# Sliding-window attention on one core: four groups of eight blocks run as one sequence of 32, with the stages of a block one block further apart

## The reference

```python
q = rms_norm((rms_norm(x, g_norm) @ w_q).reshape(b, s, 16, 64), g_q)   # 16 heads, 4 share a key head
logits = einsum("bntkgd,bnskd->bnkgts", q, k_band) * 64 ** -0.5        # 128 tokens see 256 keys
logits = where(mask, logits - slopes * dist, -inf)                     # ALiBi bias, window of 128
m = maximum(max(logits), sink)
p = exp(logits - m)
denom = sum(p) + exp(sink - m)
o = einsum("bnkgts,bnskd->bntkgd", p / denom, v_band)
x = x + o.reshape(b, s, 1024) @ w_o
```

## Time and profile before

| What | Value |
|---|---|
| median of 3 runs | 2092.54 us (2092.04 to 2097.11) |
| the profiled execution | 2095.45 us, its span 2093.5 us |
| PE busy | 2005.1 us, 96% of the span |
| DVE busy | 1400.6 us, 67% |
| ACT busy | 909.2 us, 43% |
| POOL busy | 407.5 us, 19% |
| mean granted TensorE clock | 0.986 |

### The profile page before, as it was taken

How to read it: one execution, slowest core, us unless ns; L and a number is a source line. 1 busy time by engine, 2 the same in 40 slices (tenths; PEclk the granted TensorE clock), 3 DMA queues, 4 the chain that set the end, 5 groups by cost and what they waited for, 6 DMA issues and landing times.

```text
span 2093.5 us, 29024 instructions
## 1 busy us (share of the span) xinstructions
PE 2005.1 (96%) x9968; PEld 1694.9 (81%) x9968; DVE 1400.6 (67%) x2050; ACT 909.2 (43%) x1560; POOL 407.5 (19%) x285
## 2 busy tenths in 40 slices
PE   7999899999999999999998789879899999999999
PEld 7988678788888888888998677757788888888887
DVE  5366568888887854444553777879887887853433
ACT  6233335444444443333313677746444444433332
POOL 0000001432333200001111444422333333200000
PEclk9999899999999999999999999999999999999999
DMA  4111232122221254333120000012222221254533
GB/s 165 41 51 40 71 123 98 73 89 80 80 93 68 105 219 177 131 140 111 32 69 31 11 21 10 10 61 81 81 81 79 88 92 60 110 221 150 189 139 113
DMA packets 44719, 192.96 MB, mean 92 GB/s; under 512 B 4336, under 2 KB 4464, under 8 KB 32368
## 3 DMA queue, kind: packets, MB, share of 16 engines
q1 hardware_dynamic: 44656, 192.12, 25.2%
HBM read 156.45 MB, written 35.65 MB: 92 GB/s over the span
## 4 chain that ended last, share of the span: by engine, by line
PE 84%; DVE 11%; ACT 2%; issue 2%; DMA 0%; POOL 0%; DVEq 0%; SPq 0%; ACTq 0%; POOLq 0%
PE banks L1933 28%; PE banks L1935 27%; PE banks L1934 27%; DVE lg L1847 2%; DVE t_lo L1461 1%; DVE pT_lo L1796 1%; DVE t_sum L1653 1%; DVE t_sum L1451 1%; ACT o_hi L1142 1%; DVE o_lo L1804 1%; DVE fw_lo L1443 1%; DVE small L1854 0%; DVE xT L1543 0%; DVE fw_lo L1504 0%; PE banks L2301 0%
## 5 line engine op out<-in xcount | busy, mean ns | idle before, releaser
L1933 PE MATMUL banks<-t_hi,fw_hi 128*128 128x512 f32 x1760 | 688.5, 391 | 12.7 <-issue 11.1
L1935 PE MATMUL banks<-t_hi,fw_lo 128*128 128x512 f32 x1760 | 686.1, 390 | 0.0
L1934 PE MATMUL banks<-t_lo,fw_hi 128*128 128x512 f32 x1728 | 674.0, 390 | 0.0
L1933 PEld LDWEIGHTS banks<-t_hi,fw_hi 128*128 128x128 f32 x1760 | 331.4, 188 | 86.5 <-issue 14.4
L1935 PEld LDWEIGHTS banks<-t_hi,fw_lo 128*128 128x128 f32 x1760 | 331.4, 188 | 69.1
L1934 PEld LDWEIGHTS banks<-t_lo,fw_hi 128*128 128x128 f32 x1728 | 325.2, 188 | 67.7 <-issue 0.5
L1599 DVE TENSOR_TENSOR fw_lo<-raw,fw_hi 128x512 fp32r<-128x512 f32 x120 | 84.4, 705 | 189.2 <-ACT fw_hi L979 189.2
L580 POOL TENSOR_TENSOR nrm<-raw 128x512 f32<-128x512 f32 x40 | 53.6, 1340 | 753.9 <-DVE fw_lo L1504 439.6
L932 ACT ACTIVATE xT<-xT,par 128x1024 f32<-128x1024 f32 x88 | 109.3, 1245 | 161.5 <-DVE xT L1530 119.0
L979 ACT ACTIVATE fw_hi<-raw 128x512 fp32r<-128x512 f32 x120 | 75.6, 631 | 210.6 <-PE banks L1935 210.6
L1543 DVE SCALAR_TENSOR_TENSOR xT<-xT,par 128x1023 f32<-128x1023 f32 x88 | 151.3, 1720 | 0.0
(11 more groups left out here) (184 smaller groups left out, 3647.0 us busy)
## 6 DMA issues: line engine op xcount, KB each, us to landing
raw<-in_w_f_in SPq DMA_DIRECT2D x44, 1024.0 KB, 4.8
raw<-in_w_f_out SPq DMA_DIRECT2D x44, 1024.0 KB, 4.8
c_scratch<-xT SPq DMA_DIRECT2D x44, 512.0 KB, 2.6
c_raw<-c_scratch SPq DMA_DIRECT2D x44, 512.0 KB, 5.6
w_raw<-in_w_ao SPq DMA_DIRECT2D x16, 512.0 KB, 3.4
x_scratch<-xT SPq DMA_DIRECT2D x4, 2048.0 KB, 7.4
xT<-x_scratch SPq DMA_DIRECT2D x4, 2048.0 KB, 12.9
xT<-in_x_t SPq DMA_DIRECT2D x16, 256.0 KB, 7.1
```

Source lines behind the costliest of these rows:

```text
L1933: nc.tensor.matmul(out, w_h, m_h, start=start, stop=False, **kw)
L1934: nc.tensor.matmul(out, w_h, m_l, start=False, stop=False, **kw)
L1935: return nc.tensor.matmul(out, w_l, m_h, start=False, stop=stop, **kw)
```

## The change

- The four groups are written out, and on every engine the blocks count through from 0 to 31 (`block`). The stages of block n run over the border between groups: queries of the next group are split and turned in blocks 6 and 7 of this one.
- The next group's biases are made in block 3, by ScalarE instead of VectorE, into a second buffer. Its keys are copied in block 6 (`k_twice`), transposed and split in block 7 (`keys_transpose`, `keys_upper`, `keys_lower`).
- `o_upper` and `o_lower` move by one block (n-3 instead of n-2) and to an earlier place within the block; `pT_hi` and `pT_lo` have two buffers.
- In groups 1 to 3 TensorE's `p_transpose` stands ahead of `logits`, and `weighted` is last; in group 0 it is `logits`, `p_transpose`, `weighted`. `p_transpose` has a new wait, for `pT_ready` of the block before.
- The output tiles start one block later: blocks 6 and 7 of group 0 held four, now block 7 holds two, and behind block 7 of group 3 stand three pairs and 8 tiles instead of two pairs and 8. The splits of their weights move from blocks 4 and 6 to 5 and 7.
- On VectorE one of the two additions of a block now stands behind the reciprocals; the sinks are read from the parameters and no longer copied.
- GpSimd's `v_lower` stands behind blocks 0 and 2 instead of ahead of block 0 and behind block 1.

```diff
@@ -109,7 +109,7 @@
 def step_outs(n):
 
 
-    o = (2 * n + 4) % (2 * KT)
+    o = (2 * n + 2) % (2 * KT)
...
-        pT_hi = sb("pT_hi", [P, 2, QPK * P], F32R)
-        pT_lo = sb("pT_lo", [P, 2, QPK * P], F32R)
+        pT_hi = sb("pT_hi", [P, 2, 2, QPK * P], F32R)
+        pT_lo = sb("pT_lo", [P, 2, 2, QPK * P], F32R)
+        bias_j = [bias_0, sb("bias_1", [P, QPK, 2, P], F32)]
...
+            def core(j):
                 for n in range(NCH):
-                    if n + 2 < NCH:
-                        q_lower(j, n + 2, 3)
+                    ahead = NCH * j + n + 2
+                    if ahead < NKV * NCH:
+                        q_lower(ahead // NCH, ahead % NCH, 3)
                     probabilities(n)
-                    if n == 1:
-                        v_lower(j, 1)
-                    if first:
-                        if n == 2:
-                            split(1)
-                    else:
-                        if n == 4:
-                            split(0)
-                        if n == 6:
-                            split(1)
+                    if n in (0, 2):
+                        v_lower(j, n // 2)
+                    if j == 0 and n == 2:
+                        split(1)
+                    if j and n == 5:
+                        split(0)
+                    if j and n == 7:
+                        split(1)
...
-                if first:
-                    act.wait_ge(cols_free[1], 1 + COLS_ALL)
...
+
+                for h in range(QPK):
...
                         nc.scalar.activation(lg[:, n % 2, h, b0:2, :], lg[:, n % 2, h, b0:2, :], ACT.Exp,
                                              bias=small[:, 6, h:h + 1], accum_out=small[:, 7, h:h + 1])
                     nc.scalar.activation(small[:, 7, 4:8], small[:, 6, 4:8], ACT.Exp).then_inc(exp_done, 1)
-                    if old:
-                        o_upper((n - 2) % NCH)
-                    if n == 1:
-                        v_upper(j, 1)
-                    if first and n == 2:
+                    if n + 2 < NCH or more:
+                        q_upper((block + 2) // NCH, (block + 2) % NCH)
+                    if n in (0, 2):
+                        v_upper(j, n // 2)
+                    if j == 0 and n == 2:
                         split(1)
-                    if not first:
-                        if n < 6:
+                    if j:
+                        if n < 7:
                             o_outs.add()
 
-                        if n == 4:
+                        if n == 5:
                             act.wait_ge(out_full[1], o_outs.now(-1))
                             split(0)
+                        if n == 7:
+                            act.wait_ge(out_full[1], o_outs.now())
+                    if more:
+                        if n == 3:
+                            biases(j + 1)
                         if n == 6:
-                            act.wait_ge(out_full[1], o_outs.now())
-                            split(1)
-                    if n >= 6:
+                            k_twice(j + 1)
+                        if n == 7:
+                            keys_upper()
+                    if j and n == 7:
+                        split(1)
+                    if n == 7:
                         o_outs.add()
                     blk.add()
 
-            core(0, True)
-            loop(1, NKV - 1, [(use[0], 1), (use[1], 1), (blk, NCH), (grp, 1), (o_outs, NCH)],
-                 lambda j: core(j, False))
+            act.wait_ge(consts_done, 7)
+            biases(0)
+            keys_upper()
+            q_copy(1)
+            act.wait_ge(cols_free[1], 1 + COLS_ALL)
...
             p_upper(6)
+            o_upper(5)
+            p_upper(7, 1)
+            blk.add()
             o_upper(6)
             blk.add()
-            p_upper(7)
             o_upper(7)
...
+            def keys_lower():
+
                 dve.wait_ge(kT_hi_done, grp.add())
                 nc.vector.scalar_tensor_tensor(out=kT_lo[:, :], in0=flat(0, 2), scalar=small[:, 5, 0:1],
                                                in1=kT_hi[:, :].bitcast(F32), op0=ALU.mult,
                                                op1=ALU.subtract).then_inc(kT_ready, 1)
-                if not first:
-                    add_step_outs(0, (0,))
-                if not first:
-                    o_lower(6)
+
+            def core(j):
+                sinks = par[:, COL_SINK + j * QPK:COL_SINK + (j + 1) * QPK]
...
-                    if old:
+                    if block >= 2:
                         p_lower((n - 2) % NCH)
-                    if not first or n >= 6:
-                        add_step_outs(n, (0, 1) if n else (1,))
+                    if block >= 3:
+                        o_lower((n - 3) % NCH)
+                    outs_now = j > 0 or n == 7
+                    if outs_now:
+                        add_step_outs(n, (0,))
                     dve.wait_ge(exp_done, blk.now(1))
                     link(nc.vector.tensor_tensor(small[:, 4, 8:12], sums, sink_exp, ALU.add))
                     nc.vector.reciprocal(small[:, 4 + n % 2, 16:20], small[:, 4, 8:12]).then_inc(den_done, 1)
-                    if old:
-                        o_lower((n - 2) % NCH)
+                    if outs_now:
+                        add_step_outs(n, (1,))
+                    if more and n == 7:
+                        keys_lower()
                     blk.add()
...
             p_lower(6)
+            o_lower(5)
             add_step_outs(0)
+            p_lower(7, 1)
+            blk.add()
             o_lower(6)
+            add_step_outs(1)
             blk.add()
-            p_lower(7)
-            add_step_outs(1)
             o_lower(7)
+            add_step_outs(2)
...
-            def p_transpose(m):
+            def p_transpose(m, prior=True):
 
                 pe.wait_ge(p_done, blk.now())
+                if prior:
+                    pe.wait_ge(pT_ready, blk.now(-1))
...
                 if which == 0:
-                    if n == 0 or n == 6:
-                        slot = 1 if n == 0 else 0
+                    if n == 1 or n == 7:
+                        slot = 1 if n == 1 else 0
                         pe.wait_ge(w_ready[slot], use[slot].add())
-                    if n == 6:
-                        pe.wait_ge(o_ready, blk.now(-2))
-                    if n == 2:
-                        pe.wait_ge(o_ready, blk.now(-2))
+                    if n == 3 or n == 7:
+                        pe.wait_ge(o_ready, blk.now(-3))
...
+            def keys_transpose():
+
                 pe.wait_ge(kdup_done, grp.add())
...
+
+            def core(j):
                 for n in range(NCH):
-                    if n + 1 < NCH:
+                    block, more = NCH * j + n, j + 1 < NKV
+                    last = n == NCH - 1
+                    if more or not last:
                         q_transpose(2)
-                    if (n and not first) or n >= 6:
+                    if j or last:
                         step_out(n, 0)
-                    if not first or n >= 6:
                         step_out(n, 1)
-                    if n + 1 < NCH:
+                    if last and more:
+                        pe.wait_ge(lg_done, blk.now(1))
+                        keys_transpose()
+                    if j == 0 and not last:
                         logits(n + 1, 2)
-                    if n >= 2 or (n == 1 and not first):
-                        weighted((n - 2) % NCH, not first or n > 2)
-                    if n:
-                        p_transpose(n - 1)
+                    if block:
+                        p_transpose((n - 1) % NCH, block > 1)
+                    if j and not last:
+                        logits(n + 1, 2)
+                    if block >= 2:
+                        weighted((n - 2) % NCH, 0, block > 2)
+                    if last and more:
+                        pe.wait_ge(kT_ready, grp.now())
+                        logits(0, 2)
                     blk.add()
...
             step_out(0, 0)
-            weighted(6, True)
+            step_out(0, 1)
             p_transpose(7)
-            step_out(0, 1)
+            weighted(6)
             blk.add()
             step_out(1, 0)
             step_out(1, 1)
-            weighted(7, True)
+            weighted(7)
             blk.add()
+            step_out(2, 0)
+            step_out(2, 1)
```

135 lines of the change are left out of this document (55 added, 80 removed).

## The result

The changed kernel takes **2062.64 us** (median of 4 runs, 2059.48 to 2064.11) against 2092.86 us (4 runs, 2092.04 to 2097.11) of the kernel before on the same chip: ratio 0.985, 95% interval 0.9831 to 0.9868. On another chip it was 2063.5 us against 2092.94, ratio 0.9853 (0.9837 to 0.9868). The forecast was 2060 us, with a range of 2050 to 2077. The profiled execution took 2059.48 us with a span of 2057.7.

A forecast was written before the change was run, and what follows sets the result against it. No engine is full; chains passing between engines bound each group, with most lost at group borders. Gains 16.3 + 12.0 + 0.1 + 4.7 = 33.1 us take the median 2092.54 to 2059.4, said as 2060 us; range 2050 to 2077.

The forecast's parts named there:

- The content: Groups 1 and 2: work of one group without the remaining waits, 51.1 us, with a full block at 6.41 us.
- the slack of 1.1: Groups 1 to 3: GpSimd's low parts of v and second `w_lo` end at 2.3 to 3.0 or earlier, within 1.1 us.
- The ring: Group 0: a cycle over four engines, from one reciprocal to the next, sets the pace at 5.6 us a block.
- 2.0 for v and `w_lo`: Group 0, blocks 1 and 3: 2.0 us more for the low parts of v and the weights.
- 4 at the end: End of group 0: 4 us of keys before the next group's logits.
- 1.2 for the clock: Group 0: 1.2 us taken off the gain of 13.2 us for TensorE partly at 1.2 GHz, leaving 12.0.
- the cost of 0: Block 3: the biases, 1.7 us on ScalarE, delay nothing that matters; without that cover 1.7 us a group, 5 in all.
- The first: Group 0: TensorE at 1.2 GHz throughout, 8.0 us a block, the group at its old 62 us, 2071 us; chance 0.15.
- the 8.0 of the rival: Group 0: time of a block in us if TensorE runs at 1.2 GHz, with the turn over ScalarE's copy.
- The second: All blocks: GpSimd's product falls on the negated maximum, 7.0 us a block instead of 6.4, 2072 us; chance 0.15.
- the slack of 0.3 us: Each block: GpSimd's product ends at 1.7 us, before VectorE's negated maximum asks at 2.0.
- The third: Groups 1 to 3: straight code is fetched too slowly, at 2 us a block 2107 us; chance 0.03.

The follow-up runs named there:

- The two added lines: Changed kernel; GpSimd's low parts of v (block 2) and of the weights (block 5) wait for the next block's negated maximum: 2053.35 us, ratio 0.9805.
- the added products: Changed kernel with four more unused TensorE products of 512 columns in each of blocks 0 to 6 of group 0: 2061.26 us, ratio 0.9846.

## Why the prediction was right

**Groups 1 and 2** were to save 16.3 us and saved 15.1. The content was right: full blocks at 6.41 to 6.43, the border 9.25 for 9.15, the wait for keys 0.3 for 0.4, and the wait ahead of the transposes of p in block 6 0.7 for 1.0, by the very row that was laid out, the negated maximum beside `w_lo` (it took 2.03). The step that failed is "the two low parts of v ... which is within the slack of 1.1". v's low part in block 3 held the negated maximum for 0.94 us, and the block took 6.2 instead of 5.73. That is the largest part of the 0.6 us that a group was mis-sized. The two added lines gave back this 0.5 and the 0.9 of block 6.

**Group 0** was to save 12.0 and saved 10.6. The ring was right: 5.41 us a block for 5.6, with the negated maximum at 0.81 to 0.87 in four blocks, ending with GpSimd's product. The sum over it was not. The prediction's terms (first reciprocal at 1143.4, seven blocks of 5.6, 2.0 for v and `w_lo`, 4 at the end) add up to 1188.6 and not to the 1186.7 that it states: the 2.0 were left out. Added up rightly, group 0 would have saved 11.3 less 1.2 for the clock, 10.1 us, and the whole forecast would have been 31.2. That this is the measured figure is in part luck, since its terms miss both ways. The interval with v and `w_lo` in it took 8.73 us, 3.3 more than a free one, where 2.0 was meant. From the last reciprocal to the next logits it was 2.25 us, for 4. The 1.2 for the low clock was about right: the added products show 1.0, in the block with the biases.

**Biases, split code, group 3.** Group 3 to its last logits was to gain 0.1 and lost 0.35, the same 0.5 us of v's low part. The biases on ScalarE took 1.70 us for four (forecast 1.7). In groups 1 and 2 they held nothing up. In group 0 their block still takes 6.15 us when the clock is high, 0.7 above 5.41, and ScalarE is busy for 6.11 of it: the cost of 0 does not hold there, though in the changed kernel it is hidden behind the low clock. The loop is worth 0, measured by itself.

**Tail.** Forecast: 24.7 us from the end of the logits of block 7 to the third tile and a gain of 4.7; measured 24.4 (25.32 less 0.95 for the logits themselves) and 5.05. The wait for VectorE's addition was there with 3.1 us, for 3.2.

**Sum.** 33.1 forecast, 31.2 in the attention of the profiled pair, 30.2 between the medians. By stages the gap to 31.2 is 1.2 in groups 1 and 2, 1.4 in group 0 and 0.45 in group 3, less the 0.35 that the tail did better and the 0.7 (17.10 to 16.36) between the third tile and the feed-forward part, for which nothing was forecast. In groups 1 to 3 the cause is v's low part beside the negated maximum; in group 0 it is the 2.0 that was never added, and the terms above.

**Rivals.** The first (TensorE at 1.2 GHz sets group 0's pace) had its sign, a clock of 0.80, but the clock did not stay low: the later blocks had it at 1.00 and took 5.41 us. The full block on which the low clock lay longest took 7.13 us, towards the 8.0 of the rival, and in all the low clock cost 1.0 us. The second (the product on the negated maximum in all blocks) is true of group 0, where the forecast had it in the ring, and false of groups 1 to 3: there the negated maxima of all blocks but 3 and 6 took 0.17. By the layout what decided was the slack of 0.3 us, which held. The third is excluded by the loop written out.

## What to carry to other kernels

Lay out one block per engine and close every ring that it has: which part of the change is worth what came out only of the rings. Taking back the place of `o_lo` cost 10 us and the second buffer with its order 33, where the single wait in the profile was 1.2 and 1.0. Then add the terms up twice: one of 2.0 us that was reasoned out here never reached the sum.

Before an elementwise instruction is queued on GpSimd, look for the short VectorE instruction with a chain behind it that will be issued in its time. A wait that lets the short one go first costs GpSimd, which has room, 0.8 us, and it was worth 6.5 us in the stages of this kernel. Then look for what the GpSimd instruction stands beside in its new place. A second buffer was tested here only together with the order that it allows, and is to be judged with it.

A mean clock says little of what the clock costs: look for the block in which TensorE is on the path.

## What was not expected of the hardware

- A VectorE instruction of four columns took 2.03 us (and another 2.28) beside a GpSimd product of 2.4 us, twelve to fourteen times its 0.16 to 0.17 us.
- Behind a wait of 2.6 us TensorE's granted clock was lower in two groups of three, and the block that followed took 1.3 and 1.5 us more. In group 0 a block wholly at 1.2 GHz took 5.39 us, for 5.41 of a fuller one at 2.4 GHz, while another block lost 1.0 us to the lower clock. Equal programs differ by 4.3 us (1133.30 to 1137.56) in where their attention starts, with granted clocks of 0.99 and 0.97 ahead of it.
